# Softmax loop of the last mixer: order of the turned probabilities' copies, the engines that make them, and the width of the value and compress products

## The chip, the cores and the metric

The kernel runs on one core of a Trainium2 chip. The metric is the time of one execution in device microseconds (us). A core has TensorE (matmuls; the profile calls it PE, and its weight loads PEld), VectorE (DVE), ScalarE (ACT), GpSimd (POOL) and a queue for transfers (SP). Matmul results land in PSUM, eight banks of 128 partitions by 512 columns; the other engines read them from there. All data here is fp32. TensorE's clock has two levels, 1.2 and 2.4 GHz, and the profile gives the granted one as a share: 0.50 or 1.00.

## What is computed

The reference is a long chain of layers: two blocks with mixers and expert layers, and then a last block with feed-forward layers and one mixer. The change lies in that last mixer, in its sparse attention. Cut to what matters:

```
kc = compress(k_cmp, ...);  vc = compress(v_cmp, ...)   # gelu(windows @ w1) @ w2, 31 positions
for each block of 128 queries, each head:               # 4 blocks x 8 heads, head width 64
    p_cmp = masked_softmax(q @ kc.T)                    # 31 positions
    p_slc = masked_softmax(q @ k_sel.T)                 # up to 512 positions
    p_win = masked_softmax(q @ k_win.T)                 # up to 512 positions
    o = g0 * (p_cmp @ vc) + g1 * (p_slc @ v_sel) + g2 * (p_win @ v_win)
```

The sequence here has 512 positions, so query block c sees 128 (c + 1) positions in each of the two long branches.

## The kernel before, in words

Every engine runs its own program in order; they meet through semaphores. `Banks` (`ps`) hands out the eight PSUM banks in turn: `take` gives the next bank that isn't held, `ready` waits until its last user has emptied it, `fill` and `empty` signal.

Ahead of the loop, `rest` makes the value rows (ScalarE copies them into `Mx.vp`, 64 columns each in a 320-column strip between zeroed gaps, after GpSimd has zeroed it), and `compressed(br, m)` makes the compress products: 16 matmuls with 128 x 128 weights and 62 moving columns, for br = 0, 1 and m = 0, 1. The weights of br = 1 are loaded into the slot that `rest` gives back.

The softmax loop runs over n = 0 to 17. A unit n below 16 is two heads (h = 2t, 2t + 1 with t = n // 4) of query block c = n % 4. Six items x = 0 to 5 belong to it: branch br = x % 3 (0 is the compressed one, with 31 positions; 1 and 2 are the long ones) of head x // 3.

- `scores(n)`: TensorE makes six products into six banks, in the order 0, 3, 1, 4, 2, 5 (`IN_TURN`); VectorE masks each and takes its maximum (L129); ScalarE takes the exponential and the sum (L98).
- `normal(n)`: VectorE makes the reciprocals (L120), GpSimd scales the six probability tiles in place (L111) and signals `n_p`.
- `values(n - 2)`, in the same pass n of the loop: TensorE turns each item's probabilities, 128 columns at a time (`transpose`, L95), into a bank; ScalarE copies them to SBUF (`Mx.PT`, L102, `ring<-ps` in the trace); TensorE multiplies values by them (L92, `ring,scr` and, for 31 positions, `ring 31*128`) and adds all six items in one held bank `n_o`, which ScalarE copies out (`scr<-ps 128x128`). The values are 128 columns wide: 64 of a head and 64 zeros beside them, so that the head's result lands in its half of the partitions.

ScalarE's own order in pass n is: the six exponentials of n, then the six copies of n - 2, then the output copy of n - 2. TensorE's is: the scores of n, then turns and values of n - 2 item by item, two turns ahead. VectorE and GpSimd take no part in `values`. At n = 16 four larger products (`gated`, 16 matmul records of 128x512 for each two) stand around the values of 14, two ahead and two behind. At n = 13 and 15 ScalarE has a copy of 1.89 us besides (`part_upper`). When the loop is over on all engines, the projection after it begins.

## Time and profile before

| what | value |
|---|---|
| time, median of 3 runs | 3204.3 us (3200.99 to 3208.06) |
| the profiled execution's own time | 3204.65 us |
| its span in the profile | 3202.9 us |
| mean granted clock of TensorE | 0.947 |
| busy over the span: PE, DVE, ACT, POOL | 91%, 34%, 24%, 16% |

The profile shows one execution. A matmul record is one instruction with its modelled tail, so records overlap: the time that one takes in a dense row is the row's length over its count, not its mean. An fp32 matmul leaves two records, a transpose one. A row of busy times gives start and end of the stretch, its length, then busy time and instructions of each engine, the granted clock, the DMA share and GB/s. "idle before <-releaser" is what ended the wait ahead of a row.

### The profile page before, as it was taken

The numbers are of one execution on the slowest core, as the hardware profiler recorded it, in microseconds if no ns is written. First come the engines' busy times: TensorE is split into PE (matmuls) and PEld (weight loads), VectorE is DVE, ScalarE is ACT, GpSimd is POOL, SyncE is SP. The second block draws the span as 40 slices with busy tenths as digits, with TensorE's granted clock in tenths as the row PEclk, the third lists the DMA queues.
The fourth block names the chain that finished last, engine by engine and source line by source line (L and its number), as shares of the span: only waits on it lengthen the run. The fifth ranks groups of instructions, "written<-read, shape, count | busy, mean of one in ns | idle before, by whom it ended". The sixth has DMA issues, their size and how long they took to land.

```text
span 3202.9 us, 36604 instructions
## 1 busy us (share of the span) xinstructions
PE 2926.3 (91%) x15566; PEld 2071.6 (65%) x15566; DVE 1080.1 (34%) x2032; ACT 764.3 (24%) x1365; POOL 509.1 (16%) x505
## 2 busy tenths in 40 slices
PE   6989898899969899979999988999998988999997
PEld 4777755445457665766454447888864766788886
DVE  4973210000044543320000005342388223433334
ACT  4142211011132153311101113222211355322223
POOL 0000132232210043113323311000042132000000
PEclk9989899999979999989999998999999889999998
DMA  6613899999942132369999974332310201223321
GB/s 254 208 43 118 314 386 402 407 388 399 394 150 81 53 119 82 126 230 396 411 414 405 406 297 140 104 104 88 112 48 27 96 1 53 80 92 105 97 79 55
DMA packets 143401, 621.51 MB, mean 194 GB/s; under 512 B 14447, under 2 KB 95471, under 8 KB 109568
## 3 DMA queue, kind: packets, MB, share of 16 engines
q0 software_dynamic: 40160, 403.75, 31.3%
q1 hardware_dynamic: 101920, 210.35, 19.2%
q10 hardware_dynamic: 1152, 4.98, 0.4%
q8 instruction: 127, 2.08, 0.3%
q14 instruction: 42, 0.34, 0.0%
HBM read 612.73 MB, written 29.36 MB: 200 GB/s over the span
## 4 chain that ended last, share of the span: by engine, by line
PE 72%; DMA 16%; DVE 7%; ACT 2%; issue 2%; POOL 1%; SPq 0%; DVEq 0%; POOLq 0%; ACTq 0%
PE ps L92 69%; DMA ring<-in_exp_up,wix 14%; PE ps L95 2%; DVE scr L114 1%; DVE hT L110 1%; DVE scr L106 1%; ACT hT L98 1%; DVE scr L120 1%; DMA ring<-in_mod_w 1%; DMA scr<-in_mod_w 1%; DVE ring_r L106 0%; POOL ring L135 0%; ACT scr L98 0%; DVE hT_r L106 0%; DVE scr L117 0%
## 5 line engine op out<-in xcount | busy, mean ns | idle before, releaser
L92 PE MATMUL ps<-ring,scr 128*64 128x512 f32 (+4 forms) x3392 | 750.0, 546 | 90.0 <-DMA ring<-in_exp_up,wix 65.4
L92 PE MATMUL ps<-ring_r 128*128 128x512 f32 (+1 forms) x2688 | 780.4, 377 | 29.2 <-DVE hT_r L106 21.8
L92 PEld LDWEIGHTS ps<-ring,scr 128*64 128x64 f32 (+2 forms) x3392 | 302.4, 153 | 445.4 <-issue 433.2
L92 PEld LDWEIGHTS ps<-ring_r 128*128 128x128 f32 x2688 | 498.3, 192 | 136.5 <-issue 34.2
L92 PE MATMUL ps<-hT_r,ring_r 128*128 128x512 f32 (+1 forms) x1256 | 474.5, 378 | 0.0
L92 PE MATMUL ps<-scr,ring 128*128 128x128 f32 (+1 forms) x2784 | 333.2, 282 | 21.9 <-DMA ring<-yrows 17.0
L92 PEld LDWEIGHTS ps<-scr,ring 128*128 128x128 f32 x2784 | 321.3, 195 | 31.7 <-issue 30.7
L106 DVE TENSOR_TENSOR scr<-scr,ps 64x512 f32<-64x512 f32 (+1 forms) x76 | 52.5, 690 | 777.6 <-ACT scr L98 466.1
L92 PE MATMUL ps<-scr_r,ring_r 128*128 128x512 f32 x1312 | 306.7, 390 | 0.4 <-issue 0.4
L92 PEld LDWEIGHTS ps<-scr_r,ring_r 128*128 128x128 f32 x1312 | 246.2, 188 | 52.4 <-issue 0.5
L92 PEld LDWEIGHTS ps<-hT_r,ring_r 128*128 128x128 f32 x1256 | 241.2, 192 | 43.4 <-issue 1.9
L106 DVE TENSOR_TENSOR ring_r<-ring,ring_r 128x2048 fp32r<-128x2048 f32 (+1 forms) x98 | 217.0, 2238 | 74.8 <-ACT ring_r L102 74.5
L102 ACT ACTIVATE ring_r<-ring 128x2048 fp32r<-128x2048 f32 (+1 forms) x102 | 186.3, 1834 | 180.7 <-DMA ring<-in_ffn_w 132.4
L102 ACT ACTIVATE scr<-ps 128x512 f32<-128x512 f32 (+3 forms) x216 | 110.2, 525 | 490.1 <-PE ps L92 340.9
L98 ACT ACTIVATE scr<-ps 64x512 f32<-64x512 f32 (+2 forms) x96 | 56.2, 586 | 681.7 <-PE ps L92 681.7
L92 PE MATMUL ps<-ring 128*32 128x512 f32 (+10 forms) x584 | 130.0, 488 | 26.2 <-ACT ring L102 21.3
L103 DVE COPY scr<-ps 128x512 f32<-128x512 f32 (+3 forms) x102 | 54.4, 548 | 260.9 <-PE ps L92 173.7
L95 PEld LDWEIGHTS ps<-KC,scr 64*128 64x128 f32 (+2 forms) x878 | 79.8, 140 | 94.8 <-issue 82.0
L106 DVE TENSOR_TENSOR scr<-hT,ps 128x512 f32<-128x512 f32 x44 | 30.3, 688 | 312.6 <-PE ps L92 312.6
L102 ACT ACTIVATE ring<-ps 128x512 f32<-128x512 f32 (+5 forms) x215 | 85.0, 435 | 192.4 <-PE ps L92 151.1
L92 PEld LDWEIGHTS ps<-ring 64*128 64x128 f32 (+4 forms) x584 | 76.3, 194 | 66.2 <-ACT ring L102 29.6
L95 PE MATMUL ps<-KC,scr 64*128 64x64 f32 (+2 forms) x878 | 107.7, 255 | 5.8 <-DMA scr<-hrows,scr 5.2
(148 smaller groups left out, 2560.6 us busy)
## 6 DMA issues: line engine op xcount, KB each, us to landing
ring<-in_ffn_w SPq DMA_DIRECT2D x66, 1024.0 KB, 5.6
ring<-in_mod_w SPq DMA_DIRECT2D x12, 2048.0 KB, 7.9
ring<-in_mod_w SPq DMA_DIRECT2D x16, 1024.0 KB, 5.0
ring<-in_exp_up SPq DMA_DIRECT2D x4, 2048.0 KB, 12.0
ring<-in_exp_down SPq DMA_DIRECT2D x4, 2048.0 KB, 8.8
scr<-in_mod_w SPq DMA_DIRECT2D x8, 1024.0 KB, 7.8
ring<-in_exp_gate SPq DMA_DIRECT2D x4, 2048.0 KB, 11.4
ring<-in_w_in SPq DMA_DIRECT2D x4, 2048.0 KB, 8.2
```

What stands on the lines that cost most here:

```text
L92: return self.real.matmul(o, l, r, start=start, stop=stop) if self.real else Quiet()
L95: return self.real.transpose(o, i, identity) if self.real else Quiet()
L98: return self.real.activation(o, i, f, **how) if self.real else Quiet()
L102: return self.real.activation(o, i, ACT.Copy) if self.real else Quiet()
L103: return self.real.tensor_copy(o, i) if self.real else Quiet()
L106: return self.real.tensor_tensor(o, a, b, op) if self.real else Quiet()
L110: return self.real.tensor_scalar(o, a, s1, None, op0) if self.real else Quiet()
L114: return self.real.scalar_tensor_tensor(out=o, in0=a, scalar=s, in1=b, op0=op0, op1=op1) if self.real else Quiet()
L120: return self.real.reciprocal(o, i) if self.real else Quiet()
```

## The change

It alters five things.

1. Value products are 64 columns wide. `Mx.vp` holds values without gaps (in `Mx.x`), and the two heads j = 0, 1 of a unit write partitions 64j to 64j + 64 of the output bank by turns. The zeroing of `Mx.vp` and `Mx.vcm` on GpSimd is gone.
2. The order of turns and values goes by branch: `turn(n, 0)`, `turn(n, 1)`, `values(n, 0)`, `turn(n, 2)`, `values(n, 1)`, `values(n, 2)`. The two 31-position items share one bank and one copy, so a unit takes twelve banks and not thirteen.
3. ScalarE copies the even head's turned probabilities (and the shared 31-position ones); VectorE copies the odd head's.
4. ScalarE's order in pass n: the copies of branches 0 and 1 of n - 2, the exponentials of branch 0 of n, the copy of branch 2, the exponentials of branches 1 and 2, the output copy. VectorE's: masks of branch 0, `normal(n - 1)`, masks of branch 1, copy of branch 1, masks of branch 2, copy of branch 2.
5. Compress products are made with 32-column weights, four beside each other in the four quarters of the output's partitions. `rest` copies the value rows of a tile with one instruction in place of four.

The diff, without the hunks that only rename `Mx.vp` as `Mx.readout` for other users, and those of `vcm`, which only drop its gaps:

```diff
--- before.py
+++ after.py
...
@@ -2475,10 +2475,12 @@
     Mx.C, Mx.S = (area(r_, 512) for _ in range(2))
     Mx.qT = [area(r_, 512) for _ in range(4)]
     Mx.kc, Mx.vc, Mx.ks, Mx.kw = (area(r_, 1024) for _ in range(4))
-    Mx.hid, Mx.w2s, Mx.kcm, Mx.vcm = area(r_, 248), area(r_, 512), area(r_, 62), area(r_, 320)
+    Mx.hid, Mx.w2s, Mx.kcm, Mx.vcm = area(r_, 248), area(r_, 512), area(r_, 62), area(r_, 128)
     Mx.us = area(r_, 2048)
-    Mx.PT = [Mx.us[:, 512 * i:512 * i + 512] for i in range(4)]
     Mx.x, Mx.pool_t = area(r_, 1024), area(r_, 640)
+    Mx.PT = {(br, h): Mx.us[:, 512 * i:512 * i + 512] for i, (br, h) in enumerate(((1, 0), (1, 1), (2, 0), (2, 1)))}
+    Mx.PT[0, 0], Mx.PT[0, 1] = Mx.pool_t[:, 0:128], Mx.pool_t[:, 128:256]
+    Mx.vp = Mx.x
 
     o_ = Mx.at_o
     Mx.olo = [scrR[:, o_ + 512 * i:o_ + 512 * i + 512] for i in range(4)]
...
@@ -2681,8 +2683,10 @@
             o = ps.take("cmp", br, m)
             e.wait_ge(*ps.ready("cmp", br, m))
             for p in range(16):
-                w = weights(("mix", "cmp", br), 256, p, 128 * m, 128 * m + 128)
-                x = e.matmul(o[:, 0:62], w, Mx.kp[16 * br + p], p == 0, p == 15)
+                for i in range(4):
+                    a = 128 * m + 32 * i
+                    x = e.matmul(o[32 * i:32 * i + 32, 0:62], weights(("mix", "cmp", br), 256, p, a, a + 32), Mx.kp[16 * br + p],
+                                 p == 0, p == 15)
             x.then_inc(*ps.fill("cmp", br, m))
 
         rest(0, 1, 2, 3)
@@ -2718,34 +2722,46 @@
                 e.wait_ge(*ps.ready("n_s", n, x))
                 e.matmul(o[:, 0:N], q, key, True, True).then_inc(*ps.fill("n_s", n, x))
 
-        def values(n):
-            ob = ps.take("n_o", n, hold=True)
+        def turn(n, br):
+            for j in range(2):
+                h, _, c, N, p, g, r0 = nsa(n, br + 3 * j)
+                e.wait_ge(*pool_step.of("n_p", n, br + 3 * j))
+                if br == 0:
+                    if j == 0:
+                        o = ps.take("n_t", n, 0, 0)
+                        e.wait_ge(*ps.ready("n_t", n, 0, 0))
+                    t = e.transpose(o[0:31, 128 * j:128 * j + 128], p, k("id"))
+                else:
+                    o = ps.take("n_t", n, br, j)
+                    e.wait_ge(*ps.ready("n_t", n, br, j))
+                    for a in range(0, N, 128):
+                        t = e.transpose(o[:, a:a + 128], p[:, a:a + 128], k("id"))
+                if br or j:
+                    t.then_inc(*ps.fill("n_t", n, br, j if br else 0))
+
+        def values(n, br):
+            o = ps.ap("n_o", n)
+            c, g = n % 4, n // 8
+            nk = 1 if br == 0 else c + 1
+            for j in range(2 if br else 1):
+                e.wait_ge(*ps.emptied("n_t", n, br, j))
+            for i in range(nk):
+                for j in range(2):
+                    a = 512 * (br - 1) + 128 * i + 64 * g
+                    v = Mx.vcm[0:31, 64 * g:64 * g + 64] if br == 0 else Mx.vp[:, a:a + 64]
+                    t = e.matmul(o[64 * j:64 * j + 64, 0:128], v, Mx.PT[br, j][0:31 if br == 0 else 128, 128 * i:128 * i + 128],
+                                 br == 0, br == 2 and i == nk - 1)
+            t.then_inc(*(pe_step.up("n_v", n, br) if br < 2 else ps.fill("n_o", n)))
+
+        def outputs(n):
+            ps.take("n_o", n, hold=True)
             e.wait_ge(*ps.ready("n_o", n))
-
-            def turn(x):
-                h, br, c, N, p, g, r0 = nsa(n, x)
-                K = 31 if br == 0 else 128
-                o = ps.take("n_t", n, x)
-                e.wait_ge(*ps.ready("n_t", n, x))
-                e.wait_ge(*pool_step.of("n_p", n, x))
-                for a in range(0, N, K):
-                    t = e.transpose(o[0:K, (a // K) * 128:(a // K) * 128 + 128], p[:, a:a + K], k("id"))
-                t.then_inc(*ps.fill("n_t", n, x))
-            turn(0)
-            turn(1)
-            for x in range(6):
-                if x < 4:
-                    turn(x + 2)
-                h, br, c, N, p, g, r0 = nsa(n, x)
-                nk, K = (1, 31) if br == 0 else (c + 1, 128)
-                v0 = 64 + 128 * g if h % 2 == 0 else 128 * g
-                e.wait_ge(*ps.emptied("n_t", n, x))
-                for i in range(nk):
-                    a = ((br - 1) * 4 + i) * 320 + v0
-                    v = Mx.vcm[0:31, v0:v0 + 128] if br == 0 else Mx.vp[:, a:a + 128]
-                    t = e.matmul(ob[:, 0:128], v, Mx.PT[(6 * n + x) % 4][0:K, 128 * i:128 * i + 128], x == 0 and i == 0,
-                                 x == 5 and i == nk - 1)
-                t.then_inc(*(pe_step.up("n_v", n, x) if x < 5 else ps.fill("n_o", n)))
+            turn(n, 0)
+            turn(n, 1)
+            values(n, 0)
+            turn(n, 2)
+            values(n, 1)
+            values(n, 2)
             ps.release("n_o", n)
 
         def gated(m):
...
@@ -2894,14 +2910,11 @@
             e.dma(d, I["rope"][4 + i]).then_inc(*rope_in.up("mix", i, by=16))
 
         def rest(*tiles):
-            e.wait_ge(*pool_step.of("vp_zero"))
             for i in tiles:
                 e.wait_ge(*ps.filled("mx_v", i))
                 o = ps.ap("mx_v", i)
-                for br in range(2):
-                    for g in range(2):
-                        a = (br * 4 + i) * 320 + 64 + 128 * g
-                        e.copy(Mx.vp[:, a:a + 64], o[:, br * 128 + 64 * g:br * 128 + 64 * g + 64])
+                e.copy(Mx.vp.rearrange("p (b n) -> p b n", b=2)[:, :, 128 * i:128 * i + 128],
+                       o[:, 0:256].rearrange("p (b n) -> p b n", b=2))
                 e.activation(Mx.gt[:, 24 * i:24 * i + 24], o[:, 256:280], ACT.Sigmoid).then_inc(*ps.empty("mx_v", i))
         def s5_operators(q):
             for z in range(2):
...
@@ -2955,18 +2967,20 @@
                     i = e.activation(p, p, ACT.Exp, bias=s[:, x:x + 1], scale=-1.0)
                 i.then_inc(*act_step.up("n_e", n, x))
 
-        def values(n):
-            for x in range(6):
-                h, br, c, N, p, g, r0 = nsa(n, x)
-                nk, K = (1, 31) if br == 0 else (c + 1, 128)
-                j = 6 * n + x
-                if j >= 4:
-                    b, y = divmod(j - 4, 6)
-                    e.wait_ge(*(pe_step.of("n_v", b, y) if y < 5 else ps.filled("n_o", b)))
-                e.wait_ge(*ps.filled("n_t", n, x))
-                e.copy(Mx.PT[j % 4][0:K, 0:128 * nk], ps.ap("n_t", n, x)[0:K, 0:128 * nk]).then_inc(*ps.empty("n_t", n, x))
+        def turn(n, br):
+            if n:
+                e.wait_ge(*(pe_step.of("n_v", n - 1, br) if br < 2 else ps.filled("n_o", n - 1)))
+            e.wait_ge(*ps.filled("n_t", n, br, 0))
+            if br == 0:
+                e.copy(Mx.pool_t[0:31, 0:256], ps.ap("n_t", n, 0, 0)[0:31, 0:256]).then_inc(*ps.empty("n_t", n, 0, 0))
+            else:
+                N = nsa(n, br)[3]
+                e.copy(Mx.PT[br, 0][:, 0:N], ps.ap("n_t", n, br, 0)[:, 0:N]).then_inc(*ps.empty("n_t", n, br, 0))
+
+        def outputs(n):
+            t, c = n // 4, n % 4
             e.wait_ge(*ps.filled("n_o", n))
-            e.copy(Mx.oT[h // 2][:, 128 * c:128 * c + 128], ps.ap("n_o", n)[:, 0:128]).then_inc(*ps.empty("n_o", n))
+            e.copy(Mx.oT[t][:, 128 * c:128 * c + 128], ps.ap("n_o", n)[:, 0:128]).then_inc(*ps.empty("n_o", n))
 
         def upper(t):
             e.wait_ge(*ps.emptied("n_o", 4 * t + 3))
@@ -2980,15 +2994,23 @@
             e.wait_ge(*dve_step.of("glu", m))
             e.copy(Mx.shi[m], Mx.sg[m]).then_inc(*h_hi.up("mx_out", 4 + m))
         for n in range(18):
-            if n < 16:
-                scores(n)
             if n == 16:
                 gated(0)
                 gated(1)
+            if n >= 2:
+                turn(n - 2, 0)
+                turn(n - 2, 1)
+            if n < 16:
+                scores(n, 0)
+            if n >= 2:
+                turn(n - 2, 2)
+            if n < 16:
+                scores(n, 1)
+                scores(n, 2)
             if n in (13, 15):
                 part_upper(e, ("mx_out", (n - 13) // 2))
             if n >= 2:
-                values(n - 2)
+                outputs(n - 2)
             if n in (14, 15, 16):
                 upper(n - 14)
             if n == 16:
@@ -3085,12 +3107,12 @@
                 windows(1, Mx.vc)
         turn_late((0, 3, Mx.qT[3]))
 
-        def scores(n):
+        def scores(n, br):
             s = Mx.st[:, 24 * (n % 3):24 * (n % 3) + 24]
-            if n >= 3:
-                e.wait_ge(*ps.filled("n_t", n - 3, 5))
-            for x in IN_TURN:
-                h, br, c, N, p, g, r0 = nsa(n, x)
+            if n >= 3 and br == 0:
+                e.wait_ge(*ps.filled("n_t", n - 3, 2, 1))
+            for x in (br, br + 3):
+                h, _, c, N, p, g, r0 = nsa(n, x)
                 mask = k("cmask")[:, 31 * c:31 * c + 31] if br == 0 else k("diag")[:, 512 - N:512]
                 e.wait_ge(*ps.filled("n_s", n, x))
                 e.ttr(p, ps.ap("n_s", n, x)[:, 0:N], mask, scale=-0.125, scalar=1e30, op0=ADD, op1=MIN,
@@ -3114,14 +3136,29 @@
             e.wait_ge(*h_hi.of("mx_out", i))
             e.tt(to, of, hi.bitcast(F32), SUB).then_inc(*h_lo.up("mx_out", i))
 
+        def turn(n, br):
+            if n:
+                e.wait_ge(*(pe_step.of("n_v", n - 1, br) if br < 2 else ps.filled("n_o", n - 1)))
+            N = nsa(n, br)[3]
+            e.wait_ge(*ps.filled("n_t", n, br, 1))
+            e.copy(Mx.PT[br, 1][:, 0:N], ps.ap("n_t", n, br, 1)[:, 0:N]).then_inc(*ps.empty("n_t", n, br, 1))
+
         def gated(m):
             e.wait_ge(*ps.emptied("glu", m))
             e.tt(Mx.sg[m], Mx.sg[m], Mx.y[m], MUL).then_inc(*dve_step.up("glu", m))
-        for n in range(17):
+        for n in range(18):
             if n < 16:
-                scores(n)
-            if n >= 1:
+                scores(n, 0)
+            if 1 <= n <= 16:
                 normal(n - 1)
+            if n < 16:
+                scores(n, 1)
+            if n >= 2:
+                turn(n - 2, 1)
+            if n < 16:
+                scores(n, 2)
+            if n >= 2:
+                turn(n - 2, 2)
             if n == 14:
                 part_lower(e, ("mx_out", 0))
             if n == 16:
...
@@ -3203,8 +3238,6 @@
         for q in range(4):
             s5_operators(q)
             s5_readout(q)
-        e.wait_ge(*ps.filled("s5_y", 3))
-        e.memset(Mx.vp, 0.0).then_inc(*pool_step.up("vp_zero"))
         for n in range(16):
             normal(n)
         stage_end(e, "nsa", "act", "dve", "pe")
```

## Rows read from the trace of the kernel before

**Rows 1.** Part 1 of the page: busy time, share, instructions.

```profile
PE 2926.3 (91%) x15566; PEld 2071.6 (65%) x15566; DVE 1080.1 (34%) x2032; ACT 764.3 (24%) x1365; POOL 509.1 (16%) x505
```

**Rows 2.** Busy time and clock by stage: compress products, loop to its end, all engines.

```profile
2510.20:2517.50 7.30, 7.30 (x66) 7.25 (x64) 0.00 (x0) 2.16 (x7) 0.00 (x0) 1.00 0.83 291
...
2519.20:2532.60 13.40, 13.40 (x64) 13.22 (x64) 0.00 (x0) 0.22 (x1) 0.00 (x0) 0.52 0.38 130
...
2541.20:2558.50 17.30, 14.38 (x62) 10.11 (x60) 5.81 (x32) 9.65 (x33) 8.22 (x17) 0.70 0.01 1
2558.50:2595.96 37.46, 31.71 (x193) 25.12 (x192) 10.73 (x72) 20.27 (x68) 12.39 (x24) 0.86 0.00 1
...
2633.40:2674.70 41.30, 31.38 (x194) 25.54 (x194) 16.08 (x80) 24.46 (x71) 18.34 (x28) 0.88 0.00 1
2674.70:2702.60 27.90, 26.09 (x130) 16.79 (x128) 7.17 (x11) 12.67 (x26) 1.73 (x3) 1.00 0.00 1
```

**Rows 3.** Waits of TensorE, 2541.2 to 2674.7 us: in total, times, longest.

```profile
PE ps L92 <- ACT ring L102: 19.5, 11, 4.0
```

**Rows 4.** Timeline of TensorE in pass n = 5, to the start of n = 6.

```profile
2566.27 1.79 PE L92 MATMUL ps<-ring 64*128 64x31 f32 x12
2567.99 0.29 PE L95 MATMUL ps<-KC,scr 128*31 128x128 f32 x1
...
2570.20 0.48 PE L92 MATMUL ps<-ring 31*128 31x128 f32 x2 [1.04 <-ACT ring L102]
2570.62 0.30 PE L95 MATMUL ps<-KC,scr 128*31 128x128 f32 x1
...
2573.95 2.05 PE L92 MATMUL ps<-ring,scr 128*128 128x128 f32 x16
2575.93 2.21 PE L92 MATMUL ps<-ring 64*128 64x31 f32 x12
2578.07 0.30 PE L95 MATMUL ps<-KC,scr 128*31 128x128 f32 x1
```

**Rows 5.** Timeline of TensorE, two other passes: scores, then the first turn.

```profile
2595.96 1.37 PE L92 MATMUL ps<-ring 64*128 64x31 f32 x12
2597.26 0.30 PE L95 MATMUL ps<-KC,scr 128*31 128x128 f32 x1
...
2662.48 2.64 PE L92 MATMUL ps<-ring 64*128 64x31 f32 x12
2665.05 0.30 PE L95 MATMUL ps<-KC,scr 128*31 128x128 f32 x1
```

**Rows 6.** Groups of ScalarE, 2541.2 to 2674.7 us, by form: busy, mean ns.

```profile
L98 ACT ACTIVATE hT<-hT,scr 128x512 f32<-128x512 f32 x16 | 11.4, 713 | 6.0 <-DVE scr L129 6.0
...
L98 ACT ACTIVATE scr<-scr 128x31 f32<-128x31 f32 x28 | 8.7, 319 | 5.9 <-DVE scr L129 5.8
...
L102 ACT ACTIVATE ring<-ps 128x512 f32<-128x512 f32 x12 | 6.7, 584 | 7.9 <-PE ps L95 7.9
...
L98 ACT ACTIVATE hT<-hT,scr 128x128 f32<-128x128 f32 x12 | 4.6, 386 | 0.0
L102 ACT ACTIVATE ring<-ps 128x128 f32<-128x128 f32 x16 | 3.9, 264 | 2.5 <-PE ps L95 2.3
```

**Rows 7.** TensorE's timeline where weights 64 and 32 columns wide stand beside each other.

```profile
818.36 7.09 PE L92 MATMUL ps<-ring,scr 128*64 128x512 f32 x32 [2.04 <-DMA ring<-in_exp_up,wix]
...
2470.47 1.02 PE L92 MATMUL ps<-ring,KC 128*128 128x512 f32 x2
2471.43 0.42 PE L92 MATMUL ps<-scr 128*32 128x128 f32 x8
...
2473.64 0.62 PE L92 MATMUL ps<-ring,scr 128*32 128x128 f32 x16
```

**Rows 8.** TensorE's busy time and clock in two neighbouring stretches of pass n = 6.

```profile
2578.00:2581.40 3.40, 1.35 (x9) 0.97 0.00 0
2581.40:2584.80 3.40, 3.40 (x14) 0.50 0.00 0
```

More of the change, by code:

```diff
@@ L2467, in build @@
     Mx.tmp = [s_(512), s_(512)]
-    Mx.uT, Mx.vp, Mx.gt = s_(2048), s_(2560), s_(96)
+    Mx.uT, Mx.readout, Mx.gt = s_(2048), s_(2560), s_(96)
     Mx.at_o = s_.at
@@ L2517, in build @@
     S5.W = [[Mx.sbuf[:, 2048 + 1024 * (q % 2) + 512 * z:2560 + 1024 * (q % 2) + 512 * z] for z in range(2)] for q in range(4)]
-    S5.C = [[Mx.vp[:, 1280 * (q % 2) + 640 * z:1280 * (q % 2) + 640 * z + 640] for z in range(2)] for q in range(4)]
+    S5.C = [[Mx.readout[:, 1280 * (q % 2) + 640 * z:1280 * (q % 2) + 640 * z + 640] for z in range(2)] for q in range(4)]
     S5.M = [Mx.uT[:, 512 * q:512 * q + 512] for q in range(4)]
@@ L2523, in build @@
     ffn1 = Ffn("ffn1_", lambda kt: Two.gn[:, kt:kt + 1], st_fin)
-    st_mix = Stat("mix", Mx.vp[:, 0:512], Mx.tmp, X, by_tile(8, 512), 512, None)
+    st_mix = Stat("mix", Mx.readout[:, 0:512], Mx.tmp, X, by_tile(8, 512), 512, None)
     ffn2 = Ffn("ffn2_", lambda kt: vec("n2", kt), st_mix)
@@ L2941, in act_mixer2 @@
         e.copy(Mx.kcm, ps.ap("kcm")[:, 0:62]).then_inc(*ps.empty("kcm"))
-        e.wait_ge(*pool_step.of("vcm_zero"))
         for g in range(2):
             e.wait_ge(*ps.filled("vcm", g))
-            e.copy(Mx.vcm[0:31, 64 + 128 * g:128 + 128 * g], ps.ap("vcm", g)[0:31, 0:64]).then_inc(*ps.empty("vcm", g))
-        def scores(n):
+            e.copy(Mx.vcm[0:31, 64 * g:64 * g + 64], ps.ap("vcm", g)[0:31, 0:64]).then_inc(*ps.empty("vcm", g))
+        def scores(n, br):
             s = Mx.st[:, 24 * (n % 3):24 * (n % 3) + 24]
-            for x in IN_TURN:
-                h, br, c, N, p, g, r0 = nsa(n, x)
+            for x in (br, br + 3):
+                p = nsa(n, x)[4]
                 e.wait_ge(*ps.emptied("n_s", n, x))
@@ L2990, in act_mixer2 @@
             if n >= 2:
-                values(n - 2)
+                outputs(n - 2)
             if n in (14, 15, 16):
@@ L3086, in dve_mixer2, with scores @@
         turn_late((0, 3, Mx.qT[3]))
-        def scores(n):
+        def scores(n, br):
             s = Mx.st[:, 24 * (n % 3):24 * (n % 3) + 24]
-            if n >= 3:
-                e.wait_ge(*ps.filled("n_t", n - 3, 5))
-            for x in IN_TURN:
-                h, br, c, N, p, g, r0 = nsa(n, x)
+            if n >= 3 and br == 0:
+                e.wait_ge(*ps.filled("n_t", n - 3, 2, 1))
+            for x in (br, br + 3):
+                h, _, c, N, p, g, r0 = nsa(n, x)
                 mask = k("cmask")[:, 31 * c:31 * c + 31] if br == 0 else k("diag")[:, 512 - N:512]
@@ L3154, in pool_mixer2 @@
     def pool_mixer2(e):
-        e.memset(Mx.vcm, 0.0).then_inc(*pool_step.up("vcm_zero"))
         def go(i, *key):
```

## The prediction

> **What bounds the kernel now.** Part 1 of the page first: TensorE is busy 91% of the span, nothing else over 34% [rows 1]. The change touches one stage, so the rest of the reading is there. The busy times by stage [rows 2] show the compress products (two stretches of 64 records, 7.30 us at full clock and 13.40 us at half clock), the loop from its first turn at 2541.2, and its end at 2702.6. In the loop four passes with c = 0 to 3 repeat. The cycle of n = 4 to 7 takes 37.46 us: TensorE 31.71 busy at a mean clock of 0.86, ScalarE 20.27, VectorE 10.73, GpSimd 12.39. So TensorE sets the pace, with gaps. The waits say which: up to the start of the gated products it stood 19.5 us behind ScalarE, 11 times [rows 3]. The timeline of one pass shows where [rows 4]: scores from 2566.27, two turns from 2567.99, then 1.04 us idle until ScalarE, which is busy with the exponentials of this pass, has made the first turned copy at 2570.20; from there TensorE runs densely to 2575.93. Long idle stretches cost twice: in 2578.00 to 2581.40 TensorE was busy 1.35 of 3.40 us, and the next stretch ran at 0.50 [rows 8].
>
> All that follows the loop waits for its end, and the weights that the loop's end calls for come as it ends, so what the loop gains or loses passes to the end one for one.
>
> **Prices.** At full clock:
> - Values before: 16 records of 128 columns from 2573.95 to 2575.93, 0.124 each with the edge, 0.111 within; two records of 31 positions hold 0.42 (2570.20 to 2570.62) [rows 4].
> - Weights 64 wide: 32 records of 512 moving columns in 7.09, 0.22 each; with 128 x 128 weights two such take 0.96, 0.43 each allowing for the edge [rows 7]. The two halves of the partitions thus run side by side: a 64-wide record of 128 moving columns is worth 0.0535.
> - Weights 32 wide: from 2471.43 to the end of the last row, 96 records in about 2.65 us, 0.027 each [rows 7].
> - Scores of a unit: 1.30 for c = 0, 1.72 for c = 1, 2.14 for c = 2, 2.57 for c = 3 [rows 4, 5]; two small ones of 0.43 are in each.
> - ScalarE: an exponential 0.39 to 0.71 for 128 to 512 columns, 0.32 for 31; a turned copy 0.26 to 0.58 [rows 6], in between 0.37 and 0.48 by interpolation.
>
> **Compress products.** 256 records at 0.027 are 6.9 us against 7.30 at full clock: 0.35 less for the first half, but TensorE then waits for the second half's weights, which the change leaves where they were, so this counts 0. At half clock 256 x 0.054 is 13.8 against 13.4. I take +0.4 loss as the one bound; the other is that the clock rises while it works, 5 us gained (a quarter of the records at half clock, 3.4 us, the rest twice as fast, 5.0, together 8.4 for 13.4). I take 0.3 gained, since no row shows the clock under such products. The fewer copies in `rest` and the zeroing dropped lie under the product of the next tile: ScalarE is busy 2.16 of the 7.30 us that follow; worth nothing.
>
> **TensorE's work in a pass.** With c' the query block of the unit being turned: small scores 0.43; four long scores a = 0.87, 1.29, 1.71, 2.14; the two small turns 0.25; long turns 0.44 (c' + 1), as before; 31-position values 0.45, one group in place of two; long values 8 (c' + 1) records at 0.0535, 0.43 (c' + 1), where it was 0.89 (c' + 1). A pass pairs c with c': (0, 2), (1, 3), (2, 0), (3, 1). Sums: 4.6, 5.9, 3.7, 5.0, together 19.2 in a cycle. That is far under 37.46; something else must set the pace.
>
> **The new chain.** A unit takes six score banks, one output bank and five turn banks, twelve in all, of eight. Counting on, the third score product of a pass needs the bank of the last unit's output, and that is emptied by ScalarE's output copy, now queued behind all exponentials of its pass. Let X be the moment of that copy. Then: TensorE four long scores, a; small turns and the time until ScalarE sees them 0.47; ScalarE's shared copy 0.37; its copy k of branch 1 (0.26, 0.37, 0.48, 0.58 for c' = 0 to 3); two small exponentials 0.65; copy k of branch 2, whose turns are ready by then; four long exponentials 4e (1.56, 1.98, 2.4, 2.84 for c = 0 to 3); output copy and signal 0.33. After a that is 4.3, 4.95, 4.7, 5.4. For (1, 3) TensorE's values of branch 2 end later than the exponentials, 5.1. With a: 5.2, 6.4, 6.4, 7.5, a cycle of 25.6 at full clock. VectorE's share, eight copies more in a cycle, is at ScalarE's dearest price 4.7 on top of 10.73, hidden; GpSimd's is unchanged.
>
> The same bookkeeping for n = 5 of before gives 8.9 where 9.66 was measured [rows 4], 8% short, so I take 27.6. At half clock (0, 2) and (1, 3) are as long as TensorE's own work, about twice 4.6 and 5.9, 9.1 and 11.6; (2, 0) and (3, 1) double a and the small turns and wait longer for values, 8.8 and 10.7: 40.2, with the 8% 43.4. A share f of the time at half clock then gives 27.6 / (1 - 0.364 f). The cycle of before had f = 0.28 (mean clock 0.86) [rows 2]. In the new one (2, 0) and (3, 1) leave TensorE idle about 2.7 and 2.5 us, at least as long as the gap after which the clock fell [rows 8], and the other two about 0.6. I take f = 0.3: 31.0. Bounds: f = 0 gives 27.6, f = 0.6 gives 35.3.
>
> **The sum.**
> - n = 4 to 15, three cycles: 3 x (37.46 - 31.0) = 19.4 gained. The extra 3.8 us of the last cycle (41.30 in rows 2) holds the two copies of 1.89; they delay the output copy in the same way and stay. Bounds 6.5 and 29.5.
> - n = 2, 3: 17.30 now, at a clock of 0.70. New, from the first turn: 4.7 + 7.5 less the 2.1 by which the next small scores run ahead, 10.1, 10.9 with the 8%; at f = 0.6 13.6. Gain 3.7 (1 to 5).
> - The end, 27.90 now with 14 us of gated products that stay (32 records of 512 columns at 0.43): units of c' = 2 and 3 save 1.3 and 1.8 in long values and 0.4 each in the small ones: 4 gained (2.5 to 5).
> - Compress: 0.3 (-0.4 to 5).
> - Changes of the array's shape: from 128 x 128 to 32 wide and back costs about 0.1 each [rows 7]; a small value pair between long records costs 0.2 over its two records. New is one such change per unit on the path, ahead of the 64-wide values, while one small pair less is counted above: 16 x 0.06, 1 lost (0 to 3).
>
> The Trainium skill, "TensorEngine Tiling (Array Packing)", Key Properties, says that changing the tiling mode drains TensorE. The trace agrees that a change isn't free, at about 0.1 us; if by that rule each change cost 0.2 the term would be 3 lost.
>
> Together 26.4 gained. Against the profiled execution's own 3204.65 us (its span is 3202.9; it lies 0.35 above the median of the runs) that is 3178.
>
> **The rivals.**
> - Fuller clock, 15%: denser compress products let the clock rise there, and the loop's gaps don't lower it. For: after the gap of 1.04 us the values went on at the full-clock price [rows 4]. Against: two gaps in each cycle are over 2 us. Price: 29.5 + 5 + 4 + 5 - 1 = 42 gained, 3162.
> - More half clock, f = 0.6, 8%: 6.5 + 1 + 2.5 - 1 = 9 gained, 3196.
> - The 64-wide pairs do not run side by side, 3%: 0.43 (c' + 1) more per pass, absorbed by the idle time of (2, 0) and (3, 1): 2.5 a cycle. Gain 15, 3189. Against it are the 64-wide rows [rows 7].
> - Slower than before, 5%: ScalarE's output copy behind four exponentials holds the third score bank so long, in each pass, that TensorE never keeps its full clock in the loop. Cycle 43.4, 5.9 over now: 17.8 lost, n = 2, 3 gains 0.9, the end, where the gated products keep the clock, 4: 3217. It decides from a half-clock share of 0.84; before it was 0.28. Against it: at half clock TensorE's own work nearly fills the passes (0, 2) and (1, 3), and the stage with the dense gated products ran at 1.00 [rows 2].
> - No change, 3%: between f = 0.6 and that point.
> - The forecast, 66%: 3170 to 3190.
>
> Within 0.2% (6.4 us) a measurement of this kernel cannot be told from no change. Faster by more: 0.92; within: 0.03; slower: 0.05. The range of 3160 to 3196 leaves out the slower rival, no change, half of that with more half clock and some 5% at the fast end.
>
> **What the profile of the changed kernel would show.** The loop's first turn to its end about 135 us in place of 161.4. A cycle of about 31 us, with ScalarE busy some 20 of it and no longer behind TensorE. TensorE's main wait at a score product of 64 rows (third of a pass), released by ScalarE's `scr<-ps 128x128` copy. 64-wide value records at 0.054 in dense rows. Compress records about 0.027 at full clock. It would prove me wrong if the chief wait were for VectorE or GpSimd, if TensorE's clock in the loop were below 0.75 or near 1.0, or if the value pairs stood one after the other.

## The result, and the profile after

The changed kernel takes 3154.67 us (median of 4 runs, 3148.15 to 3161.04), the kernel before 3204.07 us (3200.99 to 3208.06): a ratio of 0.9843, 95% interval 0.9824 to 0.9863. That is 49.4 us less, where 26 were forecast: right in sign, short by about half, and below the range of 3160 to 3196 us.

The profiled execution of the changed kernel is its slowest, 3161.04 us. It came to the mixer's stage 7.0 us later than the one of before, in work that the change doesn't touch, so the stage is best read by itself: from the first product of the value rows to the loop's first score, from there to the gated products, and from there to the first product of the projection. First before, then after; the columns are those of rows 2.

```profile
2495.34:2535.34 40.00, 37.83 (x205) 34.24 (x203) 1.98 (x3) 7.27 (x31) 1.50 (x1) 0.81 0.39 140
2535.34:2674.70 139.36, 115.02 (x673) 90.30 (x674) 47.70 (x290) 80.68 (x261) 51.81 (x94) 0.84 0.02 7
2674.70:2702.65 27.95, 26.10 (x131) 16.82 (x129) 7.17 (x11) 12.69 (x27) 1.73 (x3) 1.00 0.00 1
```

```profile
2502.32:2537.81 35.49, 26.29 (x589) 22.05 (x587) 1.98 (x3) 6.37 (x19) 0.00 (x0) 0.90 0.42 155
2537.81:2634.64 96.83, 81.56 (x673) 52.20 (x673) 55.22 (x315) 62.00 (x214) 46.15 (x90) 0.89 0.04 11
2634.64:2659.03 24.39, 22.46 (x130) 12.91 (x129) 11.77 (x18) 14.10 (x28) 3.75 (x6) 1.00 0.00 1
```

The stage went from 207.3 to 156.7 us: 4.5 less in the first part, 42.5 in the loop, 3.6 at its end. That is the whole difference: 50.6 us, and from the projection on both executions take 500.2 us. In the loop TensorE has as many records as before (673), but 33 us less of busy time, and it is idle less: 15.3 us in place of 24.3.

Rows of TensorE's timeline: the third score product of n = 8, then parts of passes (2, 0) and (3, 1), n = 10 and 11, and the third score product of n = 12:

```profile
2583.74 0.71 PE L92 MATMUL ps<-ring 64*128 64x128 f32 x8 [1.10 <-ACT scr L102]
...
2596.19 0.40 PE L95 MATMUL ps<-KC,scr 128*31 128x128 f32 x2
2596.43 0.38 PE L95 MATMUL ps<-KC,hT 128*128 128x128 f32 x2
2597.12 0.43 PE L92 MATMUL ps<-ring 31*64 31x128 f32 x4 [0.30 <-ACT ring L102]
...
2600.73 1.99 PE L92 MATMUL ps<-ring 64*128 64x512 f32 x8 [1.44 <-ACT scr L102]
2602.65 0.40 PE L95 MATMUL ps<-KC,scr 128*31 128x128 f32 x2
...
2604.53 0.66 PE L92 MATMUL ps<-ring 128*64 128x128 f32 x8
...
2607.83 0.71 PE L92 MATMUL ps<-ring 64*128 64x128 f32 x8 [1.10 <-ACT scr L102]
```

From the two small turns to the small values it is 0.93 us now (2596.19 to 2597.12), with 0.30 of wait, where before pass n = 5 had 1.04 of wait in 2.21 [rows 4], and n = 6, the like of n = 10, a gap of 2.05 [rows 8]. The long gap has moved to the third score product (1.44, 1.10), released by ScalarE's output copy, as foreseen. From 2583.74 to 2607.83 a cycle (four passes) takes 24.09 us; the one before it took 25.58 (from 2558.16), and the last, with ScalarE's two long copies, 26.81. Before they were 37.46, 37.44 and 41.30. The three cycles:

```profile
2558.20:2583.70 25.50, 21.78 (x192) 14.33 (x192) 13.99 (x81) 15.76 (x56) 12.47 (x24) 0.93 0.00 1
2583.70:2607.80 24.10, 20.33 (x192) 13.88 (x192) 14.08 (x81) 15.76 (x56) 12.46 (x24) 1.00 0.01 2
2607.80:2634.60 26.80, 22.70 (x188) 14.81 (x188) 15.77 (x77) 16.41 (x52) 12.46 (x24) 0.87 0.00 1
```

The clock of the first cycle is 0.93, of the second 1.00, of the third 0.87; the cycle of before ran at 0.86 [rows 2]. The length of the gap doesn't settle it. The third score product of a pass (3, 1), behind a wait of the same length and with TensorE's rows alike for 17 us before it (from 2558.16 and from 2583.74), ran almost wholly at half clock in the first cycle and at full clock in the second:

```profile
2575.15 3.48 PE L92 MATMUL ps<-ring 64*128 64x512 f32 x8 [1.43 <-ACT scr L102]
```

```profile
2575.15:2578.56 3.41, 3.41 (x8) 0.55 0.00 0
```

```profile
2600.73:2602.65 1.92, 1.92 (x9) 1.00 0.00 0
```

TensorE's waits from 2541 to 2634.6 us, beside rows 3:

```profile
PE ps L92 <- ACT scr L102: 9.8, 8, 1.9
```

And the compress products (the first starts at 2517.50):

```profile
2517.50 2.93 PE L92 MATMUL ps<-hT,ring 128*32 128x62 f32 x199
2525.26 3.73 PE L92 MATMUL ps<-hT,ring 128*32 128x62 f32 x127 [4.83 <-issue]
2529.81 2.22 PE L92 MATMUL ps<-hT,ring 128*32 128x62 f32 x128 [0.82 <-issue]
2534.92 1.04 PE L92 MATMUL ps<-hT,ring 128*32 128x62 f32 x58 [2.90 <-issue]
```

A 32-wide record takes 0.0147 us (2.93 over 199, granted clock 1.00), not 0.027; but TensorE stands idle three times for 8.6 us with no semaphore to wait for, and the weights of the second half are no longer what it waits for.

### The profile page after: what moved, and what is told of

Same layout as the page of the kernel before. It is cut to its first block, busy times and chain, and to the rows that moved or that the text cites. A ratio compares the mean times of both kernels' runs of the same rounds, so it can differ in the third digit from the quotient of the medians.

```text
span 3159.2 us, 37288 instructions
## 1 busy us (share of the span) xinstructions
PE 2880.5 (91%) x15950; PEld 2018.8 (64%) x15950; DVE 1093.0 (35%) x2064; ACT 746.5 (24%) x1305; POOL 503.9 (16%) x503
## 3 DMA queue, kind: packets, MB, share of 16 engines
q1 hardware_dynamic: 101920, 210.35, 19.4%
## 4 chain that ended last, share of the span: by engine, by line
PE 71%; DMA 17%; DVE 7%; ACT 2%; issue 2%; POOL 1%; SPq 0%; DVEq 0%; POOLq 0%; ACTq 0%
PE ps L92 69%; DMA ring<-in_exp_up,wix 15%; PE ps L95 2%; DVE scr L114 1%; DVE hT L110 1%; ACT hT L98 1%; DVE scr L106 1%; DVE scr L120 1%; DMA ring<-in_mod_w 1%; DMA scr<-in_mod_w 1%; POOL ring L135 0%; DVE hT_r L106 0%; DVE ring_r L106 0%; DVE scr L117 0%; DVE hT L114 0%
## 5 line engine op out<-in xcount | busy, mean ns | idle before, releaser
L92 PE MATMUL ps<-ring_r 128*128 128x512 f32 (+1 forms) x2688 | 780.3, 377 | 29.0 <-DVE hT_r L106 21.5
L92 PE MATMUL ps<-ring,scr 128*64 128x512 f32 (+4 forms) x3072 | 698.3, 571 | 93.1 <-DMA ring<-in_exp_up,wix 68.0
L92 PEld LDWEIGHTS ps<-ring,scr 128*64 128x64 f32 (+2 forms) x3072 | 256.2, 146 | 447.2 <-issue 436.1
L102 ACT ACTIVATE scr<-ps 128x512 f32<-128x512 f32 (+2 forms) x200 | 107.9, 548 | 459.3 <-PE ps L92 296.0
L92 PE MATMUL ps<-ring 128*64 128x128 f32 (+10 forms) x904 | 137.9, 405 | 17.2 <-ACT scr L102 9.8
L102 ACT ACTIVATE ring<-ps 128x512 f32<-128x512 f32 (+4 forms) x171 | 73.4, 464 | 211.7 <-PE ps L92 161.7
L92 PEld LDWEIGHTS ps<-ring 128*64 128x64 f32 (+4 forms) x904 | 77.5, 161 | 62.1 <-issue 35.8
```

The source lines that it names most:

```text
L92: return self.real.matmul(o, l, r, start=start, stop=stop) if self.real else Quiet()
L102: return self.real.activation(o, i, ACT.Copy) if self.real else Quiet()
```

## The experiments

Each ran beside the kernel before on one chip. "Stage" is the sum of the three stretches above, "loop" the middle one, both from the profile. Each stage is that of one profiled execution. Three kernels with the very same loop (changed, e2, e3) had loops of 96.8, 93.4 and 98.6 us at clocks of 0.89, 0.94 and 0.88, so loops that differ by up to 5 us can't be told apart. A ratio is to the runs of before beside which that kernel ran (medians 3205.82 for e1 to e4, 3204.53 for e5 to e7, 3204.51 for e8 to e11).

A cycle at a granted clock of 1.00, from one third score product with c = 0 to the next, is a finer measure: it takes 24.09 us in the changed kernel, 24.09 twice in e2 (2551.70, 2575.79, 2599.88) and 24.09 in e3 (2566.83 to 2590.92).

| kernel | median us | ratio to before, 95% | first part | loop | end | loop's clock |
|---|---|---|---|---|---|---|
| before | 3204.07 | | 40.0 | 139.4 | 28.0 | 0.84 |
| changed | 3154.67 | 0.9843 (0.9824 to 0.9863) | 35.5 | 96.8 | 24.4 | 0.89 |
| e1, 32-wide compress alone | 3207.74 | 1.001 (0.9987 to 1.0034) | 35.6 | 140.7 | 27.9 | 0.84 |
| e2, changed, compress 128 wide | 3157.2 | 0.9845 (0.9806 to 0.9884) | 40.8 | 93.4 | 24.2 | 0.94 |
| e3, changed, compress 64 wide | 3150.65 | 0.983 (0.9797 to 0.9863) | 31.9 | 98.6 | 24.2 | 0.88 |
| e4, changed, values in turn | 3152.56 | 0.9826 (0.9793 to 0.9859) | 35.1 | 99.4 | 25.0 | 0.90 |
| e5, changed, ScalarE copies all | 3159.28 | 0.9862 (0.9833 to 0.9892) | 35.0 | 102.0 | 24.2 | 0.88 |
| e6, changed, exponentials first | 3197.86 | 0.9986 (0.9968 to 1.0005) | 36.0 | 141.4 | 24.6 | 0.74 |
| e7, changed, output copy on VectorE | 3141.89 | 0.9788 (0.9756 to 0.9821) | 35.5 | 83.5 | 24.4 | 0.96 |
| e8, e7 with compress 64 wide | 3140.34 | 0.9805 (0.9785 to 0.9826) | 32.3 | 83.4 | 24.4 | 0.96 |
| e9, order alone (e4 and e5) | 3161.43 | 0.9872 (0.9849 to 0.9895) | 35.5 | 103.5 | 25.0 | 0.87 |
| e10, e6 with fillers | 3179.35 | 0.9912 (0.9886 to 0.9938) | 35.1 | 119.9 | 28.2 | 0.95 |
| e11, before with fillers | 3193.94 | 0.9967 (0.995 to 0.9984) | 39.7 | 128.2 | 30.7 | 0.95 |

**e1, compress products alone.** The kernel before, with the changed kernel's `compressed`.

```diff
-                w = weights(("mix", "cmp", br), 256, p, 128 * m, 128 * m + 128)
-                x = e.matmul(o[:, 0:62], w, Mx.kp[16 * br + p], p == 0, p == 15)
+                for i in range(4):
+                    a = 128 * m + 32 * i
+                    x = e.matmul(o[32 * i:32 * i + 32, 0:62], weights(("mix", "cmp", br), 256, p, a, a + 32), ...
```

> The kernel before with one part of the change: compress products with 32-column weights. In the changed kernel the stretch from the first product of the value rows to the loop's first score took 35.5 us where it took 40.0, though TensorE stood 8.6 us of it at 'issue'. Theory (fetch): a record costs 0.015 us, and the gaps are TensorE waiting for its own instructions, which come in packets of 16 KB; then this kernel shows the same three gaps, about 35.5 us for the stretch, and 4 to 5 us less in all, about 3200. Rival (clock): the denser products also keep TensorE's clock up in the loop behind them; then the loop's cycles of 37.46 us shorten too, by the 3.5 us that half clock cost in each, and the whole is 3190 or less.

The stage shows it: 35.6 us in the first part, with the same three gaps (4.61, 0.60 and 3.07 us), and a loop no faster (140.7). The timed runs can't show 4 us here: the medians differ by 2 the other way, with an interval of a quarter per cent (8 us) on either side. The rival falls: with denser compress products alone the loop's clock stays at 0.84.

**e2, the change without its compress products.** The same edit undone in the changed kernel.

> The changed kernel with the compress products of before (128 x 128 weights). Theory: the loop is as fast as in the changed kernel, its full cycles 24 to 26 us, and the time is 4 to 5 us above the changed kernel's 3154.7, about 3159. Rival: the loop owes its full clock to the compress stage; then its cycles rise by 3 us each and the time is 3168 or more.

The first part is 40.8 and the loop 93.4, at a clock of 0.94: the loop's gain doesn't need the narrow compress products. In time it is the changed kernel again (3157.2).

**e3, compress products 64 wide.**

```diff
-                for i in range(4):
-                    a = 128 * m + 32 * i
-                    x = e.matmul(o[32 * i:32 * i + 32, 0:62], weights(("mix", "cmp", br), 256, p, a, a + 32), ...
+                for i in range(2):
+                    a = 128 * m + 64 * i
+                    x = e.matmul(o[64 * i:64 * i + 64, 0:62], weights(("mix", "cmp", br), 256, p, a, a + 64), ...
```

> The changed kernel with compress products 64 columns wide, two beside each other: 256 matmul records where there are 512. Theory (fetch): with half the instructions the gaps at 'issue' fall from 8.6 us to under 3, and the stage ends when the second half's weights are there (about 9.5 us after the first product) and their 128 records are through, 4 us later: about 5 us less than the changed kernel, 3150. Rival: the gaps belong to the banks or to the transfers that run then, and stay: 3155.

```profile
2504.39 3.95 PE L92 MATMUL ps<-hT,ring 128*64 128x62 f32 x128
2514.03 5.20 PE L92 MATMUL ps<-hT,ring 128*64 128x62 f32 x128 [5.70 <-DMA ring<-in_cmp_w]
```

No gap at "issue" is left in these products; TensorE waits for the second half's weights alone, and the first part takes 31.9 us, 3.6 less than with 32-wide weights. The transfers of the instruction queue in the two compress stages, 32 wide (2517.5 to 2536 us) and then 64 wide (2504 to 2521 us):

```profile
q8 instruction: 4, 0.07, 1.3%
```

```profile
q8 instruction: 2, 0.03, 0.9%
```

Packets of some 0.016 MB. In the changed kernel the gaps come after 199, 127 and 128 records, inside the sums of 128 records, where no semaphore stands. Gap positions and e3 speak for the fetch; the wait itself isn't shown by any row, so this is the best supported reading, not more. Whether the weights' transfers slow the packets is open too: the 16 DMA engines were 99% busy in the first gap and 11% in the third.

**e4, value products of one head after the other's.**

```diff
-            for i in range(nk):
-                for j in range(2):
+            for j in range(2):
+                for i in range(nk):
                     a = 512 * (br - 1) + 128 * i + 64 * g
```

> The changed kernel with the 64-column value products of one head after those of the other, not by turns, so that neighbours write the same half of the partitions and can't run side by side. Theory (the order of the copies brought most): TensorE's value records cost 0.107 again, 0.43 us more for each 128 positions of a unit, of which TensorE's idle time at the score products (1.1 to 1.4 us in a pass) takes up part: 2 to 3 us a cycle more, 8 to 10 in all, 3164. Rival (the width brought most of the 12 us a cycle): 6 us a cycle more, 3175 or above.

Both expectations were too high. The whole, 3152.56 us, is no more than the changed kernel's, and the loop's 99.4 us is 0.8 above the slowest of its three likes. One reason is that the edit left much of the width's gain standing. Expected were 0.107 us a record; here are the 80 long value records of a full-clock cycle, in e4 (2577.42 to 2602.27) and then in the changed kernel (2583.74 to 2607.83):

```profile
L92 PE MATMUL ps<-ring 128*64 128x128 f32 x80 | 6.7, 282 | 0.7 <-DVE ring L103 0.7
```

```profile
L92 PE MATMUL ps<-ring 128*64 128x128 f32 x80 | 5.9, 281 | 0.7 <-DVE ring L103 0.7
```

With 128-wide values the same 80 records held TensorE for 11.2 us, read in e11, the kernel before with a cycle at full clock; there they also stand in more and shorter groups:

```profile
L92 PE MATMUL ps<-ring,scr 128*128 128x128 f32 x80 | 11.2, 279 | 0.0
```

Inside dense rows a record takes 0.111 us 128 wide, 0.072 in e4 and 0.056 in the changed kernel (the row of 44 records, 4.45 and 3.93 us from its start to the next, less 2.14 for the scores in it, over 32). So one head after the other still saves more than half of what the pairs save. The full-clock cycle gives the worth of the pairs:

```profile
2577.42:2602.27 24.85, 21.13 (x192) 14.88 (x192) 14.04 (x81) 15.95 (x56) 12.47 (x24) 1.00 0.01 2
```

That is 24.85 us against 24.09, 0.8 a cycle. What the width as a whole is worth under the new order, e4 does not say: its rival, that the width brought most, was not put to the test.

**e5, all turned copies on ScalarE.** VectorE's `turn` is gone, and ScalarE's has:

```diff
-                e.copy(Mx.PT[br, 0][:, 0:N], ps.ap("n_t", n, br, 0)[:, 0:N]).then_inc(*ps.empty("n_t", n, br, 0))
+                for j in range(2):
+                    e.wait_ge(*ps.filled("n_t", n, br, j))
+                    e.copy(Mx.PT[br, j][:, 0:N], ps.ap("n_t", n, br, j)[:, 0:N]).then_inc(*ps.empty("n_t", n, br, j))
```

> The changed kernel with the odd head's turned copies on ScalarE too (order as changed: branches 0 and 1 ahead of the exponentials, branch 2 between); VectorE makes none. ScalarE gets eight copies more in a cycle, 2 x (0.26 + 0.37 + 0.48 + 0.58) = 3.4 us. Theory (ScalarE's chain sets the cycle): all of it lands on the chain, 24 to 26 us become 28 to 29, 10 to 12 us in all, 3166. Rival (TensorE's own work sets it, the second engine is spare): no more than 1 us a cycle, 3157.

The loop is 102.0 us, 3 to 9 more than its three likes, where 10 to 12 were expected of the chain theory. The full-clock cycle is 25.45 us (2572.95 to 2598.40), 1.4 more than 24.09, with waits of up to 1.87 at the third score product. So the second engine is worth about 4 us over three cycles; the medians (3159.28 against 3154.67) lie about that far apart, but the intervals of the two ratios overlap.

**e6, ScalarE's order of before.**

```diff
-            if n >= 2:
-                turn(n - 2, 0)
-                turn(n - 2, 1)
             if n < 16:
                 scores(n, 0)
-            if n >= 2:
-                turn(n - 2, 2)
-            if n < 16:
                 scores(n, 1)
                 scores(n, 2)
...
             if n >= 2:
+                turn(n - 2, 0)
+                turn(n - 2, 1)
+                turn(n - 2, 2)
                 outputs(n - 2)
```

> The changed kernel with ScalarE's order of before: all exponentials of a pass, then the three turned copies, then the output copy. VectorE still copies for the odd head, values still stand side by side. Theory (the order is the main source, since TensorE's gap behind the exponentials is what it removed): TensorE again waits 1 to 2 us in each pass for the first turned copy, cycles of about 29 us at full clock, and the longer gaps bring half clock back: 31, some 18 us more in all, 3173. Rival (order matters little once TensorE's work is halved; the output copy, now right behind the values, frees the third score bank early): within 4 us of the changed kernel.

The whole gain of the loop is gone: 141.4 us, with 64-wide values and two copying engines in it. Expected were 18 us more; it is 45 in the loop and 43 in the whole. Its waits and one cycle:

```profile
PE ps L92 <- ACT ring L102: 40.9, 15, 4.8
```

```profile
2561.46:2599.03 37.57, 27.18 (x195) 19.39 (x193) 14.17 (x81) 16.92 (x56) 12.46 (x25) 0.77 0.01 1
```

TensorE reaches the first turned copy sooner and waits longer for the same exponentials (2.1 to 3.0 us in a pass where before had 0.9 to 2.05), and the clock is at half for 46% of the cycle. This is the mechanism that the forecast's slower rival named (gaps so long that TensorE can't keep its clock), at another place.

**e7, output copy on VectorE.**

```diff
             if n >= 2:
                 turn(n - 2, 2)
+                t, c = (n - 2) // 4, (n - 2) % 4
+                e.wait_ge(*ps.filled("n_o", n - 2))
+                e.copy(Mx.oT[t][:, 128 * c:128 * c + 128], ps.ap("n_o", n - 2)[:, 0:128]).then_inc(*ps.empty("n_o", n - 2))
```

(VectorE's loop; ScalarE's `outputs(n - 2)` is gone.)

> The changed kernel with the output copy on VectorE, right behind its turned copy of branch 2; nothing else altered. In the changed kernel TensorE's one long gap in each pass with c even or odd, 1.1 to 1.44 us, is the third score product waiting for the bank that ScalarE's output copy frees behind the exponentials. Theory: that is the chain; VectorE has the result some 1.1 us earlier, so a cycle loses 3 to 4 us, 21 in place of 24.1, 10 us in all, 3144. Rival: ScalarE's own chain sets the pace (its copies and exponentials follow each other), TensorE's gap only moves to the turned copies: same within 2 us.

3141.89 us, 12.8 below the changed kernel, loop 83.5. The waits of 1.1 to 1.44 at the third score are gone; what is left of TensorE's waits on copies from 2541 to 2612 us is small:

```profile
PE ps L92 <- DVE ring L103: 2.5, 7, 0.5
PE ps L92 <- ACT ring L102: 0.9, 3, 0.3
```

The loop's clock is 0.96. A full-clock cycle is 21.64 us (2574.93 to 2596.57, from first turn to first turn), 2.45 less, and TensorE is busy for 20.33 of it, as in the changed kernel: its own work now nearly fills the loop.

**e8, both gains.** e7 with the edit of e3.

> Both gains together: the output copy on VectorE and the compress products 64 columns wide. If they are independent, the stage (first product of the value rows to the loop's end) takes 143.3 less 3.6, about 140 us, and the whole 3138. Rival: with the compress stage shorter the loop starts at a lower clock and gives it back, 3142.

The stage is 140.0 us, as summed. The whole, 3140.34 us, is the lowest median, but can't be told from e7's 3141.89, whose ratio to before is the lower of the two.

**e9, the order alone.** The edits of e4 and e5 together.

> The changed kernel with ScalarE making all turned copies and with the value products of a head one after the other, so that of the loop's change the order (and the shared copy of the 31-position items) is all that is left. Theory (the order is nearly all of it): the stage takes 161 to 167 us where before had 207.3 and the changed kernel 156.7; the whole about 3162. Rival (width and second engine are each needed for the other's gain): the stage above 180, the whole above 3175.

Stage 164.0, loop 103.5, whole 3161.43; the full-clock cycle is 25.48 us, 1.4 above the changed kernel's. So 36 of the loop's 42.5 us stay when the second engine and the side-by-side pairs are taken away, and those two bring the other 7 together. "Order alone" says too much, though. As in e4 the values are still 64 wide, and the same 80 records take 6.8 us where 128-wide ones took 11.2; TensorE's order by branch and the shared copy of the 31-position items are in it too. With e6, what is shown is this: ScalarE's new order is needed (without it nothing of the loop's gain is left), and it brings the 36 us together with the narrow weights, TensorE's order and the shared copy. No run has the new order with 128-wide values, so how the 36 us divide between order and width is not shown. An estimate from the rows above: 80 records at 0.111 in place of 0.056 are 4.4 us more, and with the 20.33 of busy time in the changed kernel's cycle that makes 24.7, more than the whole cycle of 24.09. So the width would be worth at least 0.6 us of the 12 to 14 that a cycle lost, and more where TensorE still waits.

**e10, fillers where e6 waits.** Useless products of constants into unused columns of the output bank:

```diff
             turn(n, 0)
             turn(n, 1)
+            for _ in range(10):
+                e.matmul(ps.ap("n_o", n)[:, 256:384], k("id"), k("id"), True, True)
             values(n, 0)
```

> The kernel with all exponentials ahead of the copies, and ten products of constants (128 x 128, 0.22 us each at full clock) written to unused columns of the output bank, put where TensorE waits 2.1 to 3.0 us for the first turned copy. They add work and take no wait away. Theory (half of that kernel's loss is the clock, 0.74 in its loop, not the wait itself): the clock goes to 0.95 or more and the loop falls from 141.4 to about 115 us, 25 us in all. Rival (the waits for ScalarE set the time and the clock is only a symptom): the loop stays at 141 or grows.

Not quite the 115 expected, but more work and 21.5 us less in the loop (141.4 to 119.9), the clock at 0.95 in place of 0.74. TensorE's waits for the first copy fell from 40.9 to 9.3 us, since the fillers fill them. So about half of what e6 lost in the loop was the clock, the other half the time for which TensorE had nothing of its own to do. The end grew by 3.6, where fillers stand between dense products.

**e11, fillers in the kernel before.** Six, behind `turn(0)` and `turn(1)`.

> The kernel before with six such products of constants (1.3 us at full clock) in each pass, where TensorE waits 0.9 to 2.05 us for the first turned copy. Theory: the mean clock of its cycle goes from 0.86 to about 1.0 and 37.46 us become 33 to 34; 10 to 13 us less in all, so that some 12 us of the changed kernel's 50 are the clock's. Rival: the fillers lengthen the short waits and the cycle stays at 37.

```profile
2564.90 0.29 PE L95 MATMUL ps<-KC,scr 128*31 128x128 f32 x1
...
2598.86 0.30 PE L95 MATMUL ps<-KC,scr 128*31 128x128 f32 x1
```

```profile
2564.90:2599.50 34.60, 32.93 (x247) 27.57 (x247) 11.42 (x77) 21.32 (x71) 12.46 (x24) 1.00 0.00 1
```

From the first turn of n = 5 to that of n = 9 it is 33.96 us at a clock of 1.00, 3.5 less than 37.45. The loop is 11.2 us shorter, the end 2.7 longer. So half clock cost the loop of before at least 11 us. How much of the 42.5 us the changed kernel won back of that is not isolated, for its own loop still runs at 0.89; the rest of the 42.5 is waits that are gone and work that is less.

## Why the prediction was off

Term by term, the gain forecast and measured, in us (cycles counted from third score to third score after, from first score before; the anchors differ by about 1.5 at the front of n = 4 only):

| term | forecast | measured |
|---|---|---|
| n = 4 to 15 | 19.4 | 116.2 - 76.5 = 39.7 |
| n = 2, 3 | 3.7 | 17.3 - 15.0 = 2.3 |
| start of the loop to its first turn | 0 | 5.9 - 5.4 = 0.5 |
| end, with the gated products | 4 | 3.6 |
| compress and value rows | 0.3 | 4.5 |
| changes of shape | -1 | in the above |
| together | 26.4 | 50.6 |

The mechanism was right: ScalarE's order was what held TensorE (e6), the gap moved to the third score product, released by the output copy (the waits above, and e7), and TensorE isn't the bound of every pass any more. What failed is the size of the first term, "three cycles: 3 x (37.46 - 31.0)". A new cycle was put at 31.0 and took 25.6, 24.1 and 26.8. With the 3.8 us of the last cycle's copies that is 96.8 us for the three, where 76.5 were measured. Three steps made up the difference, two of them wrong (the surcharge of 8% and the half-clock share):

- The sum of the chain, 25.6 at full clock, was good: 24.09 was measured at 1.00. It was 1.5 high. About half of that is in passes (0, 2) and (1, 3): from the third score product of n = 8 to the first turn of n = 10 (2583.74 to 2596.19) TensorE never waits, where I had let ScalarE's chain bind. In (3, 1) long scores to the first turn took 1.92 and not 2.14.
- "8% short, so I take 27.6" was wrong. My bookkeeping fell short for n = 5 of before, a pass in which TensorE works densely but for 1.04 us, and I carried that over to a chain of ScalarE's. The full-clock cycle, 24.09, has no room for it. Where the 0.76 us of n = 5 lay, no run shows. 2.0 us a cycle.
- "I take f = 0.3" was wrong: measured 0.14 in the first cycle, 0 in the second and 0.26 in the third, against 0.28 before. This is the largest of the three. I had added up TensorE's idle time in a pass (2.7 and 2.5) and held it against a single gap of 2.05. The idle time was less (3.8 us in the whole second cycle) and in pieces, the longest 1.44 there, where before had single gaps of 1.6 and 2.05 in each cycle. 3.4 us a cycle, of which 1.5 came in the first (25.58 against 24.09) and none in the second. Why the clock fell behind 1.43 in the first and not behind 1.44 in the second stays open; that it stood at 1.00 or fell is to that extent luck of the execution. e11 confirms what half clock cost before, 3.5 a cycle.

In the last cycle ScalarE's two long copies, which I let stay in full at 3.8 us, and a clock of 0.87 together cost 2.7 over 24.09.

For the compress products, "256 records at 0.027" was the wrong price: the rows it came from had 128 moving columns, and these have 62. (Those rows give 0.029 when read from 2471.43 to the next row at 2474.18; 2.65 was 0.1 short.) The record costs 0.0147. That the row gave an upper bound alone should have widened the term's good end beyond the clock; and the idle time at no semaphore that then took over was in none of my bounds. The 64-wide pairs ran side by side about as priced: 0.056 in a dense row against 0.0535. But by e4 the pairs are worth only 0.8 us a cycle.

The rivals: fuller clock was the nearest (3162; 42 us gained, where 49 were measured): no half clock at all came true in one cycle of three, and a clock that rises from the compress products into the loop did not, as e1 and e2 show. More half clock (a share of 0.6) didn't come: the shares were 0.14, 0 and 0.26. Without ScalarE's new order it is 0.46 of a cycle (e6). That the pairs stand one after the other, a rival at 15 us gained, would have cost far less than it was priced at, as e4 shows. The rule of the Trainium skill, "TensorEngine Tiling (Array Packing)", Key Properties, that a change of mode drains TensorE, was isolated by no run: all kernels with the new order hold the same changes of shape.

## What to carry to other kernels

Where one engine makes both the long work (here exponentials) and the short copies that the busiest engine waits for, look at its order first: put the copies ahead and between, and give the one that frees a bank to an engine that is free when it is due. Narrow value products and a second copying engine without that order made TensorE's gaps longer, its clock lower, and the time the same (e6). When you undo a part to see what it is worth, read from the trace that it is undone: e4 and e9 took the pairs apart and kept most of the width's gain. Compare cycles at one granted clock, and don't forecast half clock from the length of gaps alone: the same gap had it in one cycle and not in the next. Don't carry a surcharge from one engine's work over to another's chain.

## What was not expected of the hardware

- 32-wide fp32 records with 62 moving columns follow each other at 0.0147 us at full clock (199 in 2.93), 64-wide ones at 0.031 (128 in 3.95), 128-wide ones at 0.114 (64 in 7.30). For one product of 128 columns that is 0.059, 0.062 and 0.114: here narrow weights beside each other cost about half of one wide load.
- 64-wide value records were cheaper than 128-wide ones even one head after the other: 80 in 6.7 us (e4) against 11.2 (e11), both at full clock.
- A dense run of short records stood still at no semaphore: after the first 199 the rows of 127, 128 and 58 records start 4.6 and 5.1 us apart (2525.26, 2529.81, 2534.92). At 64 wide, with half as many, there was no such gap inside the products. A tiling that multiplies the instructions can lose what it gains.
- Useless products in a gap made a kernel 0.3% faster (e11) and another 0.6% (e10 against e6, 3179.35 against 3197.86), with the loop's clock at 0.95 in both in place of 0.84 and 0.74.
